# A decoder trunk on one core: the cached key pages gathered from ScalarE's queue instead of SyncE's

## The reference: what is computed

```python
h = rms_norm(x, norm_g) * (1 + scale) + shift            # adaLN
zq, zk, zv, zqi, zki, zwi, zga, zglu, zgc, zmerge = split_in(h @ w_in)
q  = rope(rms_norm(zq)); k = rope(rms_norm(zk)); v = zv  # 8 heads, 2 kv heads, 128 wide
qi = rope(zqi); ki = rope(rms_norm(zki))                 # indexer, 16 heads, 64 wide
# samples: k_all = concat(cache_k[l][page_table], k), the same for v and ki
attn = dsa_attend(q, qi, wi, k_all, v_all, ki_all)       # top-k keys by the indexer's score
u = za * sigmoid(zb); d = causal_conv31(u); d = layer_norm(d)
out = (g_att * (attn * silu(zga)) @ w_attn_out + g_conv * (silu(d) * silu(zgc)) @ w_conv_out) @ w_out
x = x + gate * out
```

## Time and profile before

| quantity | value |
|---|---|
| median of 3 runs | 3446.49 us (3444.51 to 3449.68) |
| the profiled execution's own time | 3449.85 us |
| its span | 3448.0 us |
| PE busy | 3342.3 us (97%), 26942 matmuls |
| DVE, POOL, ACT busy | 1919.6 us (56%), 1241.7 us (36%), 1012.8 us (29%) |
| DMA, all by SP's queue but for 2272 packets | 593.10 MB, 172 GB/s |
| mean granted clock of PE | 0.986 |
| POOL's low part, mean of 472 | 2.535 us |
| a load of weights (512 KB), issue to landing | 4.0 us (median) |

### The profile page before, as it was taken

How to read it: one execution, slowest core, us unless ns; L and a number is a source line. 1 busy time by engine, 2 the same in 40 slices (tenths; PEclk the granted TensorE clock), 3 DMA queues, 4 the chain that set the end, 5 groups by cost and what they waited for, 6 DMA issues and landing times. The chain is left out here.

```text
span 3448.0 us, 66432 instructions
## 1 busy us (share of the span) xinstructions
PE 3342.3 (97%) x26942; PEld 3116.9 (90%) x26942; DVE 1919.6 (56%) x2535; ACT 1012.8 (29%) x1380; POOL 1241.7 (36%) x508
## 2 busy tenths in 40 slices
PE   6899999999999999999999999999999999999999
PEld 2699988989989989998888999999899998999998
DVE  1512668898989343332226245689999873433211
ACT  3322323232452333222223222222235423332211
POOL 0233333445423333333333333334453243334433
PEclk9899999999999999999999999999999999999999
DMA  9845444666634995658895455446665459844444
GB/s 327 278 108 123 120 119 99 159 173 167 165 103 110 269 281 179 212 192 278 294 290 157 112 127 123 110 116 163 165 174 143 117 143 271 262 161 133 130 131 95
DMA packets 880078, 593.10 MB, mean 172 GB/s; under 512 B 370972, under 2 KB 849201, under 8 KB 873787
## 3 DMA queue, kind: packets, MB, share of 16 engines
q1 hardware_dynamic: 877500, 588.58, 60.3%
q10 hardware_dynamic: 2272, 0.28, 0.1%
HBM read 546.37 MB, written 116.39 MB: 192 GB/s over the span
## 5 line engine op out<-in xcount | busy, mean ns | idle before, releaser
L879 POOL TENSOR_TENSOR w_lo_t<-raw,w_hi_t 128x1024 fp32r<-128x1024 f32 x472 | 1196.5, 2535 | 2182.2 <-ACT w_hi_t L892 2182.2
L1181 PE MATMUL acc<-act_hi,w_hi_t 128*128 128x272 f32 x6528 | 1388.2, 294 | 37.8 <-POOL w_lo_t L879 14.1
L1181 PE MATMUL acc<-act_hi,w_lo_t 128*128 128x272 f32 x6528 | 1357.2, 289 | 0.0
L1181 PE MATMUL acc<-act_lo,w_hi_t 128*128 128x272 f32 x6528 | 1353.2, 289 | 0.0
L1181 PEld LDWEIGHTS acc<-act_hi,w_hi_t 128*128 128x128 f32 x6528 | 1033.0, 189 | 98.8 <-issue 57.8
L1181 PEld LDWEIGHTS acc<-act_lo,w_hi_t 128*128 128x128 f32 x6528 | 1032.0, 190 | 0.0
L1181 PEld LDWEIGHTS acc<-act_hi,w_lo_t 128*128 128x128 f32 x6528 | 1026.6, 190 | 0.0
L892 ACT ACTIVATE w_hi_t<-raw 128x1024 fp32r<-128x1024 f32 x472 | 500.0, 1059 | 1697.2 <-PE acc L1181 1681.4
L1744 DVE SCALAR_TENSOR_TENSOR conv<-conv,cw 128x512 f32<-128x512 f32 x240 | 234.7, 978 | 22.8 <-POOL w_lo_t L879 22.8
L1645 DVE TENSOR_TENSOR stage<-stage,cs 128x544 f32<-128x544 f32 x38 | 41.1, 1082 | 336.2 <-DMA stage<-stage 336.2
L1181 PE MATMUL acc<-m_hi,w_hi_t 128*128 128x272 f32 x1024 | 215.8, 292 | 0.0
(11 more groups left out here) (241 smaller groups left out, 2460.6 us busy)
## 6 DMA issues: line engine op xcount, KB each, us to landing
raw<-in_w_in_dram SPq DMA_DIRECT2D x272, 512.0 KB, 4.0
ada_ring<-in_w_ada_dram SPq DMA_DIRECT2D x95, 512.0 KB, 7.0
raw<-in_w_in_dram SPq DMA_DIRECT2D x136, 256.0 KB, 3.3
k_near<-in_cache_k_dram SPq DMA_DIRECT2D x256, 128.0 KB
v_near<-in_cache_v_dram SPq DMA_DIRECT2D x256, 128.0 KB
k_ring<-k_near SPq DMA_DIRECT2D x64, 512.0 KB, 7.6
v_page<-v_near SPq DMA_DIRECT2D x64, 512.0 KB, 6.5
raw<-in_w_out_dram SPq DMA_DIRECT2D x64, 512.0 KB, 4.5
```

What stands on the lines that cost most here:

```text
L879: pool.tensor_tensor(w_lo_t[:, m % 2], raw[:, m % 4], w_hi_t[:, m % 2].bitcast(F32), ALU.subtract).then_inc(S.w_lo, 1)
L1181: last = pe.matmul(acc[:, 2 * m + h, 0:HALF], w[:, c % 2, k, P * m:P * m + P], r[:, kt, h * HALF:(h + 1) * HALF], start=first and k == 0 a ...
```

## The change

The key-page gather leaves SP's `aside` and becomes a function of ACT's program, called once for each chunk of groups 1 to 32 after everything else that ACT does for that chunk. The bytes, the source, the destination and the semaphore are the same; the gathers of indexer keys and of values stay on SP.

```diff
-            def gather(places, staged, keys=None):
+            def gather(places, staged):
                 for (b, g), targets in places:
                     page = sp.value_load(pages[0:1, b * PAGES + g:b * PAGES + g + 1], min_val=0, max_val=n_phys - 1)
                     for near, cache in targets:
                         sp.dma_start(near[b, g:g + 1], cache[ds(page, 1)]).then_inc(staged, 16)
-                    if keys is not None:
-                        near, cache = keys
-                        sp.dma_start(near[b, g].rearrange("h a k i -> (h a) k i"),
-                                     cache[ds(page, 1)].rearrange("y k (c i) -> (y c) k i", i=BLK)).then_inc(S.kv_staged, 16)
...
-                if 1 <= n < 33:
-                    gather([(page_at(n, i), [])], S.kv_staged, keys)
...
+            def gather_keys(l, n, i):
+
+                b, g = page_at(n, i)
+                page = act.value_load(pages[0:1, b * PAGES + g:b * PAGES + g + 1], min_val=0, max_val=n_phys - 1)
+                act.dma_start(k_near[l, b, g].rearrange("h a k i -> (h a) k i"),
+                              cache_k[l, ds(page, 1)].rearrange("y k h (a i) -> (y h a) k i", i=BLK)).then_inc(S.kv_staged, 16)
...
                         if i == 3:
                             evict(l, n, 0)
+                        if 1 <= n < 33:
+                            gather_keys(l, n, i)
```

More of the change, by code:

```diff
@@ L765, in aside @@
                     sp.dma_start(mask_t[:, :, :, :], table[:, T_MASK:N_TAB].rearrange("p (a b n) -> p a b n", a=2, b=SEQS)).then_inc(S.cs_in, 16)
-                keys, values = ((near[l], cache[l].rearrange("g p h d -> g p (h d)")) for near, cache in ((k_near, cache_k), (v_near, cache_v)))
-                if 1 <= n < 33:
-                    gather([(page_at(n, i), [])], S.kv_staged, keys)
+                values = (v_near[l], cache_v[l].rearrange("g p h d -> g p (h d)"))
                 if 1 <= n < 17:
```

## The result

The changed kernel takes 3412.9 us (median of 4 runs, 3411.59 to 3418.04), the kernel before 3447.64 us beside it (4 runs). The ratio is 0.991, with a 95% interval of 0.9898 to 0.9923. So it is faster by 34.7 us by the medians, and by 26.5 to 35.2 us by the interval. I had said 3412. The profiled execution of after took 3411.59 us with a span of 3409.8; the span before was 3448.0, so the two traces differ by 38.2 us, 3.5 more than the medians.

A forecast was written before the change was run, and what follows sets the result against it. PE's own work was taken as the bound, with stalls from SP's overfull list. Stalls 22.8 plus clock 13.1 minus ACT's cost 1.0 gave 34.9 us, so median 3412 us; forecast 3405 to 3420 (0.63), range 3400 to 3436.

The forecast's parts named there:

- The bound: Indexer-query groups: SP's list asks 27.2 us a group against PE's 24, so SP falls behind some 3 us a group.
- the rival by order: SP's queue: only the gather's place ahead of the swaps matters; moving it behind gives 3410 to 3418 us; no chance given.
- the rival by transfers: SP's DMA queue: the gather's transfers there were the bound, so idle loads leave 3413 us; no chance given.
- The signs that I named: PE's waits at L919, L922, L1250 below 2 us; clock 1.00; SP waits for POOL some 50 us; swaps within 6 us.
- Stalls and clock: PE's waits for `stage` and before the transposes give back 22.8 us; the low clock following stalls gives 13.1.
- The one stall that I left in part: PE's wait before the transposes (L1250), 9.0 us in two layers: 8.0 back, 0.5 left in each layer.
- Half the gain: Rival, chance 0.16: the stall before the transposes stays, set by DVE's 16.6 us chain; 18.9 us gained, 3427.6 us.
- ACT's cost: Softmax groups 29 to 32: gathers of 1.75 us make `hi` 0.7 us late, costing 0.5 us a layer, 1.0 in all.
- the slower rival: Chance 0.07: ACT bounds the softmax groups, +20 us, 3466 us; decides from 1.1 us passed on per gather.
- more than I say: Rival, chance 0.08: PE's waits for POOL in the convolution groups shift away too, some 8 to 11 us more, 3402.
- no change: Rival, chance 0.06: the swaps are late by what the DMA engines do; 3446 us.

The follow-up runs named there:

- the idle loads: Changed kernel plus two, three or four unused page-number loads on SP per chunk of groups 1 to 16, no transfer added: 3412.07, 3410.1, 3451.01 us.
- the gather behind the swaps: Against the kernel before: key gather stays on SP but is issued behind its chunk's swaps; 3450.5 us, ratio 1.0015 to the kernel before.
- the four loads: Changed kernel plus four unused page-number loads on SP per chunk of groups 1 to 16, no transfer added: 3451.01 us, ratio 1.0016 to before.
- the version with two gathers: Against the changed kernel: ACT gathers each key page twice in groups 1 to 11, SP gathers from group 12 on; 3423.87 us, ratio 0.9953 to before.
- the version with ACT to group 11: Against the changed kernel: ACT issues key gathers only in groups 1 to 11, SP those of 12 to 32; 3412.73 us, again 3411.25 us.

## Why the prediction was right, step by step

**The bound.** Right, and shown by the idle loads: SP's list was longer than PE's group, 27.2 against 24 us, and the nine stalls were its backlog. The window views and the queue's waits had said it before; the rival by order fell with the gather behind the swaps, the rival by transfers with the four loads. The signs that I named came: SP waits 84.3 us where I had asked for 50, swaps are issued 5.9 us after the eviction, and there is no new wait for `pt_p` or `probs_p`.

**Stalls and clock.** I had 22.8 us for the stalls and 13.1 for the clock, 35.9; the two stretches of groups 1 to 11 became 20.6 + 17.6 = 38.1 us shorter (unrounded). Of these 23.8 are the waits themselves and 14.3 are left for the clock, inside my bounds of 10.7 and 15.1. The clock can be read by itself too: in windows of 1 us, 30.7 us of these two stretches of the kernel before have a granted clock of 0.50 and none of after. In 3.5 of them PE stood anyway, and half of the other 27.2, 13.6 us, is lost, which leaves 0.7 unexplained. Not every stall brought the low clock: it came with those of 2.78, 3.04, 3.35 and twice 4.51 us, and not with those of 0.39, 1.90 and twice 1.67. The one stall that I left in part (0.5 us in each layer before the transposes) went entirely. DVE's last rotation in after:

```profile
406.96 0.72 DVE L1648 TENSOR_TENSOR stage<-stage,cs 128x544 f32<-128x544 f32 x1 [11.73 <-DMA stage<-stage]
407.60 0.72 DVE L1649 TENSOR_TENSOR stage<-stage,cs 128x544 f32<-128x544 f32 x1
...
419.70 1.42 DVE L1657 TENSOR_TENSOR q_att<-stage 128x544 f32<-128x544 f32 x1
```

It runs 14.2 us (406.96 to 421.12) where it ran 16.6: the product of 2.90 us is 0.72 here, as I had allowed for with "2 us and more". PE comes to the transposes at 422.75, so the chain has 1.6 us to spare. "Half the gain" (the chain sets the stall) was thus not far off: it failed by 1.6 us. But a short chain alone isn't enough. With the gather behind the swaps it ran only 14.1 us (426.07 to 440.19), and PE still stood 4.6, because the swaps were late.

**ACT's cost.** This term was mis-sized: I said 1.0 us in all, it is 3.1 (2.0 and 1.1) in this profile, and 4.1 in the second profile of after and in the three versions with idle loads, which have the same gathers there. Two numbers were off. A gather takes ACT's queue about 2.0 us, not 1.75 (two in a row, in the version with two gathers, are issued 2.04 us apart), since the issue itself is longer there. Its lines in after, and SP's for the same new form in the version with ACT to group 11 (ns min/median/max):

```profile
L964 ACTq TENSOR_LOAD <-pages x256: 441/447/1063, 157.1 to 2726.1; - x128
...
L965 ACTq DMA_DIRECT2D k_near<-in_cache_k_dram x256: 1143/1152/3731, 158.0 to 2727.0; - x128
```

```profile
L765 SPq TENSOR_LOAD <-pages x168: 263/278/935, 429.2 to 2720.8; - x168
...
L766 SPq DMA_DIRECT2D k_near<-in_cache_k_dram x168: 775/787/973, 429.9 to 2721.5; - x168
```

I had taken SP's 0.79 for ACT, on the word of four small issues; it is 1.15. Second, `hi` came up to 1.0 us late and not 0.7. ACT in group 30 of after:

```profile
929.34 0.51 ACT L1038 ACTIVATE probs_p<-probs_p,npeak_p 128x256 f32<-128x256 f32 x1
...
930.17 1.15 ACTq L965 DMA_DIRECT2D k_near<-in_cache_k_dram  x1
930.24 0.19 ACT L1038 ACTIVATION_READ_ACCUMULATOR probs_p<-probs_p,npeak_p 128x1 f32 x1
931.42 1.06 ACT L886 ACTIVATE w_hi_t<-raw 128x1024 fp32r<-128x1024 f32 x1 [0.99 <-issue]
```

The mechanism is as said: the issue at 930.17 runs beside the exponentials, whose last part starts at 930.24, and only its rest, 0.99 us, is in front of `hi`. PE's waits for ACT's gate eviction and for `q_att` grew by 1.1 and 1.0 us over both layers; the longest for the gate was 1.1 and is 1.3, and two of the four for `q_att` are new. What passes on is 3.1 to 4.1 us for 32 gathers, 0.1 us each, far from the 1.1 from which the slower rival would have decided. In groups 1 to 28 the cost is nothing, as said, but the version with two gathers shows that this cover has an end, and that it is thinnest in group 1, which I hadn't looked at.

**What I did not have in the sum.** Some 3.2 us net come from outside these stretches: -1.8 between chunks 49 and 116, -2.7 between 130 and 240, +1.3 behind 366. The -2.7 lie in one place, chunks 200 to 210, and no version that was profiled has them as long as the kernel before, the one with the gather behind the swaps included (-2.8), so they are no effect of the change. Of the -1.8 most is in group 20. PE waits 2.86 us for POOL in both traces, and before a low clock follows it while after none does. The windows just behind the stall, before and after:

```profile
685.00:692.00 7.00, 6.18 (x37) 6.18 (x38) 6.20 (x7) 0.00 (x0) 3.10 (x2) 0.76 0.63 176
```

```profile
664.00:672.00 8.00, 6.81 (x54) 6.81 (x55) 6.83 (x8) 0.43 (x1) 3.48 (x2) 1.00 0.77 191
```

That is 1.55 us. It is no effect of the change either: in other versions, again the one with the gather behind the swaps among them, groups 19 and 20 are 4.5 us shorter than in the kernel before, and 1.9 of these come back in the two groups behind them. So "more than I say" did not come true as a mechanism, and it is this part, not the stalls, by which the traces differ more than the medians. Sum by medians: 34.7 us against my 34.9, in which the clock and the stalls were 2.2 too small, ACT's cost 2.1 too small, and the rest is the spread of single executions. That these two errors cancel, and the sum lies within 0.2 us of the medians, is luck. One slip in words: the range leaves out "no change" and "slower", which are not the last two rivals of the list.

**The rule that spoke against it.** The Trainium skill (DMA: Bandwidth & Descriptors, "Issuing engines are not separate DMA queues") says that another issuing engine saves only the issuing time. The four idle loads show just that, since SP's time alone, with no transfer, brings the loss back. The Trainium skill also calls this time usually small beside the DMA. For this gather it isn't: the issue took 0.79 us on SP, and the transfer itself would fill all 16 DMA engines for some 0.85 us, an estimate from the packets of ACT's queue in after (6.4% of 3409.8 us, for 256 gathers); how long one takes to land, the profile doesn't say. What decided was not that ratio, but that SP's list was longer than PE's group. The Trainium skill (Perfetto Trace Analysis, "What DMA-bound means") names a sequencer full of issuing as a bound of its own. The trace agrees, with one addition: more than half of the 2.04 us a page were register loads and waits for them, which are no DMA slices.

## What to carry to other kernels

An issuing engine has no busy number on a profile page; read its waits instead. If it waits for almost nothing over a stage (1.3 us in 245), add up its list for a group and compare it with what PE needs. Here it was 27.2 against 24 us: taking 2 us out of each cycle was worth the whole backlog downstream, and a new order within the cycle was worth nothing. Move the work to an engine that idles at that stage, only for the stage that needs it, and look at what stands behind it there: here ACT's idle time covered one gather for each chunk, not two, and not quite one in the softmax.

## What the hardware showed that I had not expected

- The same DMA instruction takes 0.79 us to issue on SP and 1.15 us on ACT, and a page-number load 0.28 and 0.45 us.
- An issue on ACT took 3.73 us in after and up to 4.63 us in another version, where the median is 1.15. It was the second one behind SP's 832 KB copy, and all ten such ended 7.5 to 7.8 us after that copy's issue.
- The same stall of PE for POOL (2.86 us) is followed by some 3.4 us at 1.2 GHz in the profile before (a mean clock of 0.76 over 7.00 us), and by no drop in the one after.
- Page-number loads on SP start 0.53 us apart when four stand in a row, though the load itself has a median of 0.267 us there: the register arithmetic behind it has 0.147, the check of bounds 0.018, and some 0.1 us stands in no row.
